# Two more pairs of tiles by seven products in each of the first two up stages, and their preparation put in another order

## The reference

```python
D_MODEL, SEQ, D_FF = 1024, 512, 2816
def swiglu_ffn(h, w_in, w_out):
    gate, up = jnp.split(jnp.einsum('bsd,df->bsf', h, w_in), 2, axis=-1)
    return jnp.einsum('bsf,fd->bsd', jax.nn.silu(gate) * up, w_out)
# in layer 0 and 1 of the first block:
hn = rmsnorm(h, norm_gains[layer, 2])
h = h + rmsnorm(swiglu_ffn(hn, ffn_w_in[layer], ffn_w_out[layer]), norm_gains[layer, 3])
```

## Time and profile before

| what | value |
|---|---|
| median of 3 runs | 2322.04 us (2321.7 to 2323.33) |
| profiled execution, first to last instruction | 2320.9 us |
| profiled execution's own time | not on the page; 1.1 us lie between its span and the median |
| TensorE busy | 2309.1 us, 99% |
| VectorE busy | 1498.3 us, 65% |
| ScalarE busy | 1119.0 us, 48% |
| GpSimd busy | 223.6 us, 10% |
| granted TensorE clock | 1.000 |

### The profile page before, as it was taken

The page is one execution under the profiler, slowest core; times in us unless marked ns, Lnnn a source line. Parts: engine busy times, 40 slices in busy tenths (PEclk is TensorE's granted clock), DMA queues, the critical chain, the costliest instruction groups (busy, mean ns, idle before and its releaser), DMA issues.

```text
span 2320.9 us, 32131 instructions
## 1 busy us (share of the span) xinstructions
PE 2309.1 (99%) x12088; PEld 1950.9 (84%) x12088; DVE 1498.3 (65%) x2173; ACT 1119.0 (48%) x1829; POOL 223.6 (10%) x313
## 2 busy tenths in 40 slices
PE   9999999999999999999999999999999999999999
PEld 8777889988888888999888778888888878888887
DVE  6665789952738968899428876777434456777731
ACT  6655544452539965445326854444323444544420
POOL 1221013200125410232000000000001000000000
PEclk9999999999999999999999999999999999999999
DMA  5433223332242222333322223323322323233232
GB/s 167 152 132 102 85 92 109 104 112 93 87 118 64 64 84 82 99 110 111 113 89 77 64 82 91 100 90 106 100 93 91 100 69 95 91 100 100 95 107 79
DMA packets 72541, 226.30 MB, mean 98 GB/s; under 512 B 7921, under 2 KB 19489, under 8 KB 72417
## 3 DMA queue, kind: packets, MB, share of 16 engines
q1 hardware_dynamic: 67840, 210.72, 28.5%
q0 software_dynamic: 4576, 13.89, 1.9%
HBM read 221.28 MB, written 2.18 MB: 96 GB/s over the span
## 4 chain that ended last, share of the span: by engine, by line
PE 92%; DVE 3%; ACT 3%; POOL 1%; issue 1%; DMA 0%; DVEq 0%; ACTq 0%; SPq 0%
PE bank L338 26%; PE bank L340 25%; PE bank L339 25%; PE bank L478 5%; PE bank L470 4%; PE bank L1605 1%; PE bank L1596 1%; PE bank L1639 1%; DVE w_lo L312 0%; DVE h L756 0%; POOL hgrn_lv L2560 0%; PE bank L2651 0%; PE bank L2015 0%; POOL hgrn_lv L2547 0%; PE bank L3103 0%
## 5 line engine op out<-in xcount | busy, mean ns | idle before, releaser
L312 DVE TENSOR_TENSOR w_lo<-raw,w_hi 128x1024 fp32r<-128x1024 f32 (+1 forms) x310 | 402.3, 1308 | 218.4 <-ACT w_hi L307 218.1
L338 PE MATMUL bank<-x_hi,w_hi 128*128 128x512 f32 x1344 | 529.2, 394 | 1.2 <-ACT sb_q L2761 1.0
L340 PE MATMUL bank<-x_hi,w_lo 128*128 128x512 f32 x1344 | 523.4, 389 | 0.0
L339 PE MATMUL bank<-x_lo,w_hi 128*128 128x512 f32 x1344 | 523.1, 389 | 0.0
L307 ACT ACTIVATE w_hi<-raw 128x1024 fp32r<-128x1024 f32 (+1 forms) x310 | 344.6, 1121 | 179.9 <-PE bank L340 93.5
L338 PEld LDWEIGHTS bank<-x_hi,w_hi 128*128 128x128 f32 x1344 | 252.3, 188 | 57.4 <-issue 3.1
L340 PEld LDWEIGHTS bank<-x_hi,w_lo 128*128 128x128 f32 x1344 | 252.2, 188 | 53.0
L339 PEld LDWEIGHTS bank<-x_lo,w_hi 128*128 128x128 f32 x1344 | 252.5, 188 | 51.2 <-issue 0.5
L338 PE MATMUL bank<-st_a_hi,w_hi 128*128 128x512 f32 (+1 forms) x396 | 145.1, 366 | 0.0
L340 PE MATMUL bank<-st_a_hi,w_lo 128*128 128x512 f32 (+1 forms) x396 | 144.7, 365 | 0.0
L1374 DVE TENSOR_TENSOR bank<-bank,rstd 128x512 f32<-128x512 f32 x120 | 83.2, 696 | 92.2 <-PE bank L340 92.2
(11 more groups left out here) (444 smaller groups left out, 4673.2 us busy)
## 6 DMA issues: line engine op xcount, KB each, us to landing
raw<-in_w_up SPq DMA_DIRECT2D x120, 512.0 KB, 3.5
raw<-in_w_down SPq DMA_DIRECT2D x64, 704.0 KB, 4.2
st_raw_even<-in_w_up SPq DMA_DIRECT2D x28, 512.0 KB, 4.2
st_raw_odd<-in_w_up SPq DMA_DIRECT2D x24, 512.0 KB, 4.0
raw<-in_w_fox_qk SPq DMA_DIRECT2D x16, 512.0 KB, 3.7
raw<-in_w_hgrn_qf SPq DMA_DIRECT2D x16, 512.0 KB, 3.5
fox_c_keys_a<-fox_c_rows POOLq DMA_DIRECT2D x8, 640.0 KB, 4.1
fox_c_keys_b<-fox_c_rows POOLq DMA_DIRECT2D x8, 640.0 KB, 4.5
```

The costliest lines, as they stand in the source:

```text
L312: nc.vector.tensor_tensor(w_lo[:, slot, 0:size], raw[:, slot % 2, 0:size], w_hi[:, slot, 0:size].bitcast(F32), ALU.subtract).then_inc(sem( ...
L338: nc.tensor.matmul(out, w[0], x[0], start=first, stop=False)
L339: nc.tensor.matmul(out, w[0], x[1], start=False, stop=False)
L340: return nc.tensor.matmul(out, w[1], x[0], start=False, stop=last)
```

## The change

The number of plain tiles falls from 8 to 6, and that of seven-product pairs rises from 14 to 16, in each of the two stages. st_xn moves to tiles 6 to 13, and st_mix from the place of st_sum to tiles 14 and 15. Tiles 4 and 5, in banks 4 to 7 which pair 0 uses as well, are now the last plain ones.

The order of the preparation is written anew. TensorE waits for each form's low part in front of its product, no longer for all seven, and before product 3 of pair 0 for the gate of tile 5. On VectorE forms 3 and 4 stand behind the gate of tile 3; low parts 0 and 3, form 2 and low parts 1, 4 and 2 around the gate of tile 4; "a", the first sum, low part 5, "s12" and form 6 ahead of the scale of tile 5's second bank; "s3", the second sum, low part 6, "g" and "s4" behind its gate. ScalarE converts units 10 and 11 ahead of the forms. GpSimd's first sum of pair 0 no longer waits for the low parts. SP's text is the same.

```diff
-        ST_ALL = 2 * (FT - 8)
+        ST_ALL = 2 * (FT - 6)
...
-        st_mix = nc.alloc_sbuf_tensor_at("st_mix", [P, QUAD, PAIR_T], F32, offset=at_sq)
+        st_mix = nc.alloc_sbuf_tensor_at("st_mix", [P, QUAD, PAIR_T], F32, offset=arena + 4 * T * (ST_FIRST + DT))
...
             def part(i, out):
+                if not n:
+                    pe.wait_ge(sem("st_xlo"), 7 * f + ORDER_X.index(i) + 1)
...
-            if not n:
-                pe.wait_ge(sem("st_xlo"), 7 * f + 7)
-            pe.wait_ge(sem("gated_ready"), FT * f + (ST_FIRST + n - 2 if n > 1 else 5 + 2 * n) + 1 + 2)
+            pe.wait_ge(sem("gated_ready"), FT * f + ST_FIRST + n - 2 + 1 + 2)
...
+            if not n:
+                pe.wait_ge(sem("gated_ready"), FT * f + ST_FIRST - 1 + 1 + 2)
             part(3, acc[3])
...
-            for j in (1, 2, 3):
+            for j in range(1, ST_FIRST // 2 if f < 2 else 4):
...
-                        if ft == 7:
-                            act_forms(act, f, (6,))
+                        if ft < ST_FIRST - 2:
+                            up_ahead(convert_act, act, f, j, 2 * p, u, last)
+                        if ft == ST_FIRST - 1:
                             act.wait_ge(sem("unit_used"), u + 2 + CREDIT)
                             act_pair(act, f, 0, "a")
-                            act_pair(act, f, 0, "s12")
+                            act_forms(act, f, (5,))
...
-                        up_ahead(convert_act, act, f, j, 2 * p + 1, u, last)
-                        if ft == 4:
-                            act_forms(act, f, (0, 3))
-                        if ft == 5:
-                            act_forms(act, f, (1, 4))
-                        if ft == 6:
-                            act_forms(act, f, (2, 5))
-                        if ft == 7:
+                        if ft < ST_FIRST - 2:
+                            up_ahead(convert_act, act, f, j, 2 * p + 1, u, last)
+                        if ft == ST_FIRST - 3:
+                            up_ahead(convert_act, act, f, j + 1, 0, u + 4, last)
+                            up_ahead(convert_act, act, f, j + 1, 1, u + 4, last)
+                            act_forms(act, f, (0, 3, 1))
+                        if ft == ST_FIRST - 2:
+                            act_forms(act, f, (4, 2))
+                        if ft == ST_FIRST - 1:
                             used(act, u + 2)
+                            act_pair(act, f, 0, "s12")
                             act_pair(act, f, 0, "s3")
+                            act_forms(act, f, (6,))
                             act_pair(act, f, 0, "g")
                             act_pair(act, f, 0, "s4")
...
                 if n:
                     pool.wait_ge(sem("st_lo"), 5 * (g - 1) + 2)
-                else:
-                    pool.wait_ge(sem("st_xlo"), 7 * f + 7)
...
-                        if ft == 7:
-                            dve_sums(dve, f, 0, True)
-                            dve_pair(dve, f, 0, "s3")
-                            dve_pair(dve, f, 0, "g")
-                            dve_pair(dve, f, 0, "s4")
...
-                        if ft == 4:
-                            dve_forms(dve, f, 3)
-                            dve_forms(dve, f, 4)
+                        if ft == ST_FIRST - 2:
                             dve_form_lo(dve, f, 0)
                             dve_form_lo(dve, f, 3)
-                        if ft == 5:
-                            dve_forms(dve, f, 2)
-                            dve_form_lo(dve, f, 1)
-                            dve_form_lo(dve, f, 4)
-                        if ft == 6:
-                            dve_form_lo(dve, f, 2)
+                        if ft == ST_FIRST - 1:
+                            dve_pair(dve, f, 0, "a")
+                            dve_sums(dve, f, 0, False)
+                            dve_form_lo(dve, f, 5)
+                            dve_pair(dve, f, 0, "s12")
                             dve_forms(dve, f, 6)
-                            dve_form_lo(dve, f, 5)
                         scale(1)
...
                     nc.vector.tensor_tensor(out, silu[:, p, :], second, ALU.mult).then_inc(sem("gated_ready"), 1)
-                    if f < 2 and ft == 6:
+                    if f < 2 and ft == ST_FIRST - 3:
+                        dve_forms(dve, f, 3)
+                        dve_forms(dve, f, 4)
+                    if f < 2 and ft == ST_FIRST - 2:
+                        dve_forms(dve, f, 2)
+                        dve_form_lo(dve, f, 1)
+                        dve_form_lo(dve, f, 4)
+                        dve_form_lo(dve, f, 2)
+                    if f < 2 and ft == ST_FIRST - 1:
+                        dve_pair(dve, f, 0, "s3")
+                        dve_sums(dve, f, 0, True)
                         dve_form_lo(dve, f, 6)
-                        dve_pair(dve, f, 0, "a")
-                        dve_sums(dve, f, 0, False)
-                        dve_pair(dve, f, 0, "s12")
+                        dve_pair(dve, f, 0, "g")
+                        dve_pair(dve, f, 0, "s4")
```

More of the change, by code:

```diff
@@ L251, in build @@
         st_sum = nc.alloc_sbuf_tensor_at("st_sum", [P, 2, T], F32, offset=at_sq)
-        st_mix = nc.alloc_sbuf_tensor_at("st_mix", [P, QUAD, PAIR_T], F32, offset=at_sq)
+        st_mix = nc.alloc_sbuf_tensor_at("st_mix", [P, QUAD, PAIR_T], F32, offset=arena + 4 * T * (ST_FIRST + DT))
+        assert ST_FIRST + DT + 2 <= A_MAIN
         def st_raw_pair(n):
@@ L1156, in up_body @@
                     if f < 2:
-                        up_ahead(convert_act, act, f, j, 2 * p, u, last)
-                        if ft == 7:
-                            act_forms(act, f, (6,))
+                        if ft < ST_FIRST - 2:
+                            up_ahead(convert_act, act, f, j, 2 * p, u, last)
+                        if ft == ST_FIRST - 1:
                             act.wait_ge(sem("unit_used"), u + 2 + CREDIT)
                             act_pair(act, f, 0, "a")
-                            act_pair(act, f, 0, "s12")
+                            act_forms(act, f, (5,))
                         act.wait_ge(sem("gated_ready"), n + 1)
```

## The result

The changed kernel takes **2332.33 us** (median of 5, 2331.57 to 2332.81) against 2322.24 before: a ratio of 1.0042, 95% interval 1.0031 to 1.0053. It is 10.1 us slower, where 10.2 were forecast. The profiled span is 2330.9 us, 10.0 more than before.

The account below looks back on a forecast made before the run. TensorE, busy 99% of the span, was taken as the bound. Per stage 6.2 + 0.5 − 1.6 = 5.1, for two 10.2; 2320.9 + 10.2 + 1.1 = 2332.2 us, own range 2330 to 2334, 8 in 10 2326.6 to 2336.

Parts of the forecast that it names:

- Term 1: TensorE's own work: a seven-product pair costs 10.08 us against 10.88 plain, a gain of 1.60 us a stage.
- Term 2: Preparation of the forms on VectorE: two early GpSimd sums among the low parts hold VectorE back 2.2 us.
- the edits put at nothing: ScalarE's conversions of units 10 and 11 ahead of its forms, and the wait per product: no cost.
- Term 3: Pair 0: TensorE waits 0.6 us for the gate of tile 5 and 0.6 for the last block.
- Term 4: Pair 1, fetched late behind low part 6: waits of 2.0, 2.4 and 0.6 us; whole hold 6.2 a stage.
- The tail: Start of the down stage: VectorE's low parts come 1.2 us later, so 0.5 us a stage is lost.
- The clock: Rival: TensorE's clock falls after its waits; one pair at 1.2 GHz in each stage adds 20 us: 2352; chance 0.04.
- GpSimd's early sums cost nothing: Rival: GpSimd's early sums don't delay VectorE, pair 0 has no wait: +5.8 us, 2327.8; chance 0.15.
- The fetch is hidden: Rival: pair 1's fetch is covered, kernel faster; 2318.8 us with no wait at all; chance 0.11, wholly or in part.
- Slower landing: Rival: fetches land half a microsecond later and one more VectorE operation is blocked a stage: 2335.4 us; chance 0.10.

Follow-up runs that it names:

- experiment 2: The changed kernel, with the two sums that GpSimd made for pair 0 made by VectorE; the fetch of pair 1 stays late: 2330.39 us.
- Experiment 3: The kernel before, with one SP wait changed so that pair 1 is fetched only when all blocks of pair 0 are made: 2329.99 us.
- experiment 1: The changed kernel, with pair 1 fetched early into the place of the later odd pairs, once the last plain unit is computed: 2328.75 us.
- experiment 6: The changed kernel with the early fetch of pair 1, plus 20 extra matmuls with overwritten result before product 5 of pair 0: 2326.07 us.
- experiment 5: The changed kernel with early fetch of pair 1, pair 0's sums on VectorE and low part 6 behind "s4": 2322.19 us.
- 7: The changed kernel with early fetch of pair 1, low part 6 behind "s4", and the sums of pairs 0 and 1 on VectorE: 2320.09 us.
- 4: The changed kernel with both the early fetch of pair 1 and pair 0's sums on VectorE: 2325.55 us.

## Why the prediction was right, and where it was lucky

**Term 1** (1.60 us a stage): right. The pairs from 2 on are 10.08 us apart, as before ((477.42 − 336.25)/14). One remark beside it was wrong: an eighth of the columns of a pair is worth 1.36 us and 0.80 were gained, so less than half of the saving went into the shorter matmuls, and not most of it.

**Term 2** (GpSimd's sums cost VectorE 2.2 us): right, and shown by experiment 2. Low parts 1, 4 and 2 took 5.7 us instead of 3.5; low part 1 began at 301.76, forecast 301.66, so the edits put at nothing cost nothing up to there; low part 6 ended at 317.07, forecast 316.9.

**Term 3** (pair 0 held 0.6 + 0.6): right, 0.61 and 0.67 from start to start.

**Term 4** (the fetch of pair 1): right in every step. Issue 317.15 (317.0), first product 323.18 (323.05), third 328.38 (328.3), gate of pair 0 at 336.16 (336.1), hold 6.2 (6.2). The waits in pair 1 were 1.97, 2.32 and 0.58, forecast 2.0, 2.4 and 0.6. Experiment 3 shows the late fetch alone as a cause, and 1 that without it the waits of pair 1 are gone. What the prediction didn't say is what an early fetch alone would meet: GpSimd's sums of pair 1 then fall on pair 0's last blocks. Undoing the late fetch gives 3.6 us back, undoing the sums 1.9, and undoing both 6.8. The early fetch gave so little alone because of the clock: with TensorE kept busy (experiment 6) it gives 6.3. Only with low part 6 and pair 1's sums moved too does the change pay.

**The tail** (0.5 us a stage): right in the first stage, wrong in the second. In the first, VectorE's lead at pair 15 was 467.34 − 460.79 = 6.6 us (6.4 forecast). Tile 9's low part was done at 483.20 + 0.68 = 483.9, 0.3 after TensorE's turn (6.15 us into the stage), and the first down stage was 0.5 us longer from its first matmul to its last, 121.90 us against 121.36. In the second it was 121.40: TensorE had been held 1.1 us more, so VectorE's lead at pair 15 was 7.2 us and tile 9's low part came 0.3 ahead of TensorE's turn.

**The clock.** This was put aside as a rival at 2352. Its mechanism did act, in one stage of the two and at about 1 us, not the 10 us of a whole pair (the hold was 7.3 us instead of 6.2, and 0.15 of the difference stood there before the clock fell). So the closeness of the sum is in part luck. By the starts of the down stages the change cost 4.7 us in the first stage and 5.7 in the second, where 4.6 and 4.6 were forecast; the tails cost 0.6 instead of 1.0; and the rest of the span is 1.0 shorter, which no edit explains: 10.0. The tail of the second stage is no independent piece of luck: the same low clock that lengthened the hold gave VectorE the time that the tail needed. TensorE: Matmul & The Clock Gate (the Trainium skill), Part 1, has the fall of an idle engine's clock; experiment 6 shows it here by taking the idleness away (2.5 us less with 40 more matmuls).

**The rivals.** "GpSimd's early sums cost nothing" falls with experiment 2. "The fetch is hidden" falls with the trace; its limit (a hold under 1.6 us a stage decides) held: with 1.5 in experiment 5 the kernel ties with the one before, with 0.4 to 0.6 in 7 it is just faster. "Slower landing" didn't occur: from the issue of pair 1 to GpSimd's sum there were 4.87 us in the first stage and 5.06 in the second, where 4.83 were taken.

Left open: why the clock fell in one stage and not in the other behind waits of nearly the same length. Length alone doesn't decide it: the clock fell behind a wait of 1.75 us in experiment 2 and stayed at 1.00 behind 1.9 us in the first stage of 3 and 2.3 in the first stage of 4. No run varied a wait's length or place alone.

## What to carry to other kernels

Where a stage is started earlier, list every transfer that its first two rounds need and what each waits for: a buffer laid over another tile turns the last reader of that tile into the start of a fetch, and from there to the block's use stood 11 us here (4.9 to the landing, 6.3 through three engines), which an earlier start can silently take. When a wait is removed from GpSimd, ask what of VectorE it will now run beside. And a hole of 2 us on TensorE can cost more than 2 us: look at the clock of the stretch behind it.

## What the hardware showed that was not expected

- TensorE's granted clock fell behind waits as short as 1.75 us (0.50 in the window shown in experiment 2); it was 0.56 over 3.8 us in the changed kernel's second stage and 0.50 over 6 us in experiment 1. It did so behind some waits and not behind others of the same length, and cost nothing to 2.6 us a time. In none of the nine profiles did it fall behind the wait of 1.6 us of the earlier trace rows.
- A GpSimd addition gets in between two queued VectorE operations. Low part 1 lasted 1.22 us, but low parts 4 and 2, beside the additions that began at 301.77 and 304.09, took 2.32 and 2.31. The ends in the rows fit with each addition taking its turn after the VectorE operation then running, and the next one of VectorE standing until it had ended. Two sums cost VectorE 2.2 us, more than the 1.2 us in which it makes them itself.
